# The residual sum of a layer stays in its PSUM bank; ScalarE copies it to x, and VectorE multiplies the bank with the scale row

## What is computed

```
def rmsnorm(x, g):
    y = x * rsqrt(mean(x * x, -1) + 1e-6) ; return y * g

for l in range(2):
    sh1, sc1, g1, sh2, sc2, g2 = split(silu(c) @ ada_w[l] + ada_b[l], 6)
    h = rmsnorm(x, norm1_g[l]) * (1 + sc1) + sh1
    x = x + g1 * hybrid_mixer(h, ...)        # ends with y @ w_out
    h = rmsnorm(x, norm2_g[l]) * (1 + sc2) + sh2
    x = x + g2 * swiglu(h, ...)              # ends with (...) @ w_ffn_out
return rmsnorm(x, final_g)
```

## Time and profile before

| | us |
|---|---|
| median of 3 runs | 1493.08 (1492.28 to 1493.75) |
| profiled execution, its own time | 1497.33 |
| its span in the trace | 1495.5 |
| TensorE busy | 1457.5 (97% of the span) |
| GpSimd busy | 1203.5 (80%) |
| VectorE busy | 785.5 (53%) |
| ScalarE busy | 739.3 (49%) |

### The profile page before, as it was taken

The page is one execution under the profiler, slowest core; times in us unless marked ns, Lnnn a source line. Parts: engine busy times, 40 slices in busy tenths (PEclk is TensorE's granted clock), DMA queues, the critical chain, the costliest instruction groups (busy, mean ns, idle before and its releaser), DMA issues.

```text
span 1495.5 us, 21644 instructions
## 1 busy us (share of the span) xinstructions
PE 1457.5 (97%) x7666; PEld 1218.3 (81%) x7666; DVE 785.5 (53%) x1582; ACT 739.3 (49%) x1222; POOL 1203.5 (80%) x968
## 2 busy tenths in 40 slices
PE   7999999999999999999999999999999999999997
PEld 3898777799977987778788887878888887788886
DVE  7667754766658758745466204264650043655302
ACT  3335675544444444764544445464654345455431
POOL 4799989888887977559898988907999977279994
PEclk9999999999999999999999999999999999999999
DMA  9995557688874996337666565714556757155651
GB/s 357 387 335 176 177 170 229 214 300 310 304 267 138 398 320 191 107 102 228 219 237 202 194 200 168 227 52 146 192 190 198 218 154 225 43 169 198 197 193 60
DMA packets 149685, 313.87 MB, mean 210 GB/s; under 512 B 10933, under 2 KB 31817, under 8 KB 149577
## 3 DMA queue, kind: packets, MB, share of 16 engines
q1 hardware_dynamic: 147824, 311.15, 62.1%
q10 hardware_dynamic: 1754, 1.35, 0.3%
HBM read 311.39 MB, written 1.06 MB: 209 GB/s over the span
## 4 chain that ended last, share of the span: by engine, by line
PE 86%; DVE 9%; ACT 2%; issue 1%; POOL 1%; DMA 0%; SPq 0%; DVEq 0%; ACTq 0%
PE bank L720 53%; PE bank L763 12%; PE bank L764 8%; PE bank L761 5%; DVE bank L1606 2%; PE bank L949 1%; PE bank L928 1%; POOL lo_units L676 1%; PE bank L965 1%; ACT hi_units L1190 1%; PE bank L908 1%; PE bank L799 1%; DVE bank L1527 1%; PE bank L851 1%; PE bank L1000 0%
## 5 line engine op out<-in xcount | busy, mean ns | idle before, releaser
L676 POOL TENSOR_TENSOR lo_units<-raw_units,hi_units 128x512 fp32r<-128x512 f32 (+3 forms) x928 | 1153.5, 1277 | 257.0 <-ACT hi_units L1190 255.9
L1190 ACT ACTIVATE hi_units<-raw_units 128x1024 fp32r<-128x1024 f32 (+1 forms) x470 | 483.3, 1031 | 437.3 <-PE bank L720 276.4
L720 PE MATMUL bank<-hi_units,turned 128*128 128x512 f32 (+3 forms) x1600 | 439.9, 390 | 1.5 <-DVE turned L1575 1.2
L720 PEld LDWEIGHTS bank<-hi_units,turned 128*128 128x128 f32 x1600 | 294.0, 189 | 53.0 <-issue 2.5
L764 PE MATMUL bank<-turned,lo_units 128*128 128x256 f32 x1024 | 288.2, 281 | 0.0
L720 PE MATMUL bank<-hi_units,turned_wide 128*128 128x512 f32 x992 | 275.5, 392 | 0.0
L763 PE MATMUL bank<-turned,hi_units 128*128 128x512 f32 x736 | 260.6, 399 | 0.0
L720 PE MATMUL bank<-lo_units,turned 128*128 128x512 f32 (+3 forms) x800 | 253.7, 384 | 1.5 <-POOL lo_units L676 1.3
L720 PEld LDWEIGHTS bank<-hi_units,turned_wide 128*128 128x128 f32 x992 | 185.8, 188 | 38.7 <-issue 0.5
L764 PEld LDWEIGHTS bank<-turned,lo_units 128*128 128x128 f32 x1024 | 194.2, 190 | 0.2
L720 PEld LDWEIGHTS bank<-lo_units,turned 128*128 128x128 f32 x800 | 150.4, 189 | 31.6 <-POOL lo_units L676 4.8
(11 more groups left out here) (253 smaller groups left out, 1385.0 us busy)
## 6 DMA issues: line engine op xcount, KB each, us to landing
ada_units<-in_ada_w SPq DMA_DIRECT2D x88, 512.0 KB, 8.1
raw_units<-in_w_ffn_tiles SPq DMA_DIRECT2D x72, 512.0 KB, 5.3
raw_units<-in_mlp_w_out SPq DMA_DIRECT2D x64, 512.0 KB, 3.3
raw_units<-in_mlp_w_tiles SPq DMA_DIRECT2D x56, 512.0 KB, 3.3
raw_units<-in_w_in SPq DMA_DIRECT2D x56, 458.0 KB, 9.3
raw_units<-in_w_in SPq DMA_DIRECT2D x48, 512.0 KB, 6.1
raw_units<-in_w_ffn_out SPq DMA_DIRECT2D x44, 512.0 KB, 3.7
raw_units<-in_moba_w_qkv SPq DMA_DIRECT2D x24, 512.0 KB, 3.8
```

What stands on the lines that cost most here:

```text
L676: pool.tensor_tensor(LO[:, s, b, 0:w], RAW[:, u["slot"], b, 0:w], HI_[:, s, b, 0:w].bitcast(F32), ALU.subtract).then_inc(lo_ready.sem, lo_ ...
L720: ins = pe.matmul(BANK[2 * c["pair"] + t][:, 0:w], (A[a] if A is BT else A[:, a])[:, part, t * P:(t + 1) * P], W[:, s, b, 0:w], start=(i = ...
L1190: act.activation(HI_[:, s, 0:n, 0:w], RAW[:, u["slot"], 0:n, 0:w], ACT.Copy)\
```

## The change

In the three boundaries A, B and C the residual sum is written to the PSUM bank instead of to x in SBUF. ScalarE squares the bank (not x) and copies the bank to x with an activation of its own (`keep_rows`). The product with the scale row reads bank and scale row. For the first half it is written in place and waits until ScalarE has copied. For the second half it is written to bank `TP`, now for both row tiles behind the addition of the squares; ScalarE's copy waits for this product (both read the bank), and stands between `root` and `prep` in ScalarE's list. TensorE's wait for the second pair (by then due a whole product later) is for this product and for the copy. Boundary D does the same work as before.

```diff
@@ tensor: pair_free
+            if what in ("wout", "ffo") and half == [1]:
+                pe.wait_ge(drained.sem, drained.at((*c["before"], 1)))
+                pe.wait_ge(act_side.sem, act_side.at(("kept", ("n2", i) if what == "wout" else ("n1", i + 1), 1, 1)))
+                return
@@ scalar
+        def keep_rows(tag, half, banks, tiles):
+            for t in tiles:
+                act.activation(X[:, t, half * CW:(half + 1) * CW], banks[t][:, :], ACT.Copy)\
+                    .then_inc(act_side.sem, act_side.mark(("kept", tag, half, t)))
@@ scalar: across_norm
-                    squares(tag, 1, (rows, ("x", key, t)), (t,), pair_banks(key) if tag == "final" else None)
+                    squares(tag, 1, (rows, ("x", key, t)), (t,), pair_banks(key))
                     root((tag, t), RSTD[:, t:t + 1], STAT[:, t:t + 1], 0, 1.0 / D)
+                    if tag != "final":
+                        act.wait_ge(drained.sem, drained.at((*key, t)))
+                        keep_rows(tag, 1, pair_banks(key), (t,))
@@ scalar: the first half (and the same for ffo, when a layer follows)
-            squares(("n2", l), 0, (drained, ("wout", l, 0)))
+            squares(("n2", l), 0, (drained, ("wout", l, 0)), banks=pair_banks(("wout", l, 0)))
+            keep_rows(("n2", l), 0, pair_banks(("wout", l, 0)), range(NT))
@@ vector: across_rms
-                bank, xs = pair_banks(key)[t][:, :], X[:, t, CW:2 * CW]
-                say(v.tensor_tensor(bank if coef is None else xs, xs, bank, ALU.add), ("x", key, t))
+                bank = pair_banks(key)[t][:, :]
+                say(v.tensor_tensor(bank, X[:, t, CW:2 * CW], bank, ALU.add), ("x", key, t))
...
-                if t:
-                    add_squares()
-                if coef is not None:
-                    ins = v.tensor_tensor(second[:, :], X[:, t, CW:2 * CW], MOD[:, coef + CW:coef + 2 * CW], ALU.mult)
-                    if t:
-                        tell(ins, drained, key)
-                    else:
-                        link(ins)
                 if t == 0:
                     dve.wait_ge(act_side.sem, act_side.at(("squares", tag, 0)))
-                    add_squares()
+                add_squares()
+                if coef is not None:
+                    ins = v.tensor_tensor(BANK[TP][:, :], second[:, :], MOD[:, coef + CW:coef + 2 * CW], ALU.mult)
+                    tell(ins, drained, (*key, t))
                 reciprocal_root(tag, t)
-                for half, bank in ((0, first), (1, second)):
+                for half, bank in ((0, first), (1, second if coef is None else BANK[TP])):
@@ vector: add_to_x
-                    ins = v.tensor_tensor(banks[t][:, :] if coef is None else xs, xs, banks[t][:, :], ALU.add)
+                    ins = v.tensor_tensor(banks[t][:, :], X[:, t, cc * CW:(cc + 1) * CW], banks[t][:, :], ALU.add)
                 tell(ins, drained, key)
                 after(key)
                 if coef is not None:
-                    scaled(cc, coef, to=banks)
+                    for t in range(NT):
+                        dve.wait_ge(act_side.sem, act_side.at(("kept", tag, cc, t)))
+                        ins = v.tensor_tensor(banks[t][:, :], banks[t][:, :], MOD[:, coef + cc * CW:coef + (cc + 1) * CW], ALU.mult)
+                    link(ins)
```

More of the change, by code:

```diff
@@ L595, in _ @@
                 if (l, c, i) == (1, 6, 0):
-                    sp.wait_ge(drained.sem, drained.at(("ffo", 0, 1)))
+                    sp.wait_ge(drained.sem, drained.at(("ffo", 0, 1, 1)))
                 if (l, c, i) in ((0, 10, 0), (1, 10, 0)):
@@ L1431, in _ @@
             prep_chunk(("ffo", l, 0))
-            squares(following, 0, (drained, ("ffo", l, 0)), banks=pair_banks(("ffo", l, 0)) if l + 1 == DEPTH else None)
+            squares(following, 0, (drained, ("ffo", l, 0)), banks=pair_banks(("ffo", l, 0)))
+            if l + 1 < DEPTH:
+                keep_rows(following, 0, pair_banks(("ffo", l, 0)), range(NT))
             across_norm(("ffo", l, 1), following, True, following if l + 1 < DEPTH else ("x", 0))
@@ L1600, in turn_lo_tile @@
                                  part[:, :, 0, :].bitcast(F32), ALU.subtract), turned_lo, (tag, "tile", n))
-        def scaled(half, coef, tiles=range(NT), to=None):
-            for t in tiles:
-                cols = slice(half * CW, (half + 1) * CW)
-                ins = v.tensor_tensor(to[t][:, :] if to else O[:, t, cols], X[:, t, cols], MOD[:, coef + half * CW:coef + (half + 1) * CW], ALU.mult)
-            link(ins)
         def root_of_squares(tag):
@@ L1991, in _, with add_to_x @@
             turn_lo(("y", l), AT, part=slice(2, 4))
-            def add_to_x(key, gain, factor, coef):
+            def add_to_x(key, gain, factor, tag, coef):
                 cc = key[-1]
@@ L2001, in add_to_x @@
                 for t in range(NT):
-                    xs = X[:, t, cc * CW:(cc + 1) * CW]
-                    ins = v.tensor_tensor(banks[t][:, :] if coef is None else xs, xs, banks[t][:, :], ALU.add)
+                    ins = v.tensor_tensor(banks[t][:, :], X[:, t, cc * CW:(cc + 1) * CW], banks[t][:, :], ALU.add)
                 tell(ins, drained, key)
@@ L2006, in add_to_x @@
                 if coef is not None:
-                    scaled(cc, coef, to=banks)
-            add_to_x(("wout", l, 0), 2 * D, 0.5, 4 * D)
+                    for t in range(NT):
+                        dve.wait_ge(act_side.sem, act_side.at(("kept", tag, cc, t)))
+                        ins = v.tensor_tensor(banks[t][:, :], banks[t][:, :], MOD[:, coef + cc * CW:coef + (cc + 1) * CW], ALU.mult)
+                    link(ins)
+            add_to_x(("wout", l, 0), 2 * D, 0.5, ("n2", l), 4 * D)
             across_rms(("wout", l, 1), 2 * D, 0.5, ("n2", l), 4 * D, 3 * D, ("n2", l))
@@ L2047, in _ @@
             following = ("n1", l + 1) if more else "final"
-            add_to_x(("ffo", l, 0), 5 * D, 1.0, D if more else None)
+            add_to_x(("ffo", l, 0), 5 * D, 1.0, following, D if more else None)
             across_rms(("ffo", l, 1), 5 * D, 1.0, following, D if more else None, 0,
```

## The result

The changed kernel takes 1497.22 us (median of 18 runs, 1494.07 to 1501.1); the kernel before, on the same chip and in turn with it, takes 1493.62 us (18 runs, 1490.3 to 1497.36). The ratio is 1.0023, with a 95% interval of 1.0014 to 1.0032: 3.4 us slower (2.1 to 4.8), where +0.1 us was forecast. The profiled execution took 1495.27 us, its span is 1493.5 us. That is less than the 1497.33 us of the profiled execution of before, although the median is more: one pair of profiles shows the opposite of what the timed runs show. This is the riddle of the case.

The account below looks back on a forecast made before the run. TensorE, busy 97% of the span, was taken as the bound. A 0.6 us lost, C 1.9 lost and B 2.4 gained gave +0.1 us, so a median of 1493.2 us, range 1489.5 to 1496.6.

Parts of the forecast that it names:

- the term for B: At boundary B, the net of earlier start, faster clock and added delays: 2.4 us gained.
- Part 1: Product reading a bank isn't held by GpSimd, 0.70 us each: gain 1.4 us at A, 2.6 at B, 0.1 at C.
- Rival 4: Product of bank and row is held by GpSimd too; boundaries lose about 2 us each: 1499 us; chance 0.02.
- Part 2: At B, with the 2.57 us wait cut, TensorE runs at 2.4 instead of 1.2 GHz: 1.55 us more gain.
- Parts 3 and 4: At tile 0, root to `o_rows` grows by 0.34 us; ScalarE's copy makes the next high part 1.02 us later.
- Part 5: The addition of tile 1's squares misses a GpSimd gap, 1.05 us at A and C; r is tile 0's root start.
- Rival 1: Tile 1's addition slips into the earlier GpSimd gap: A and C 1.05 us better each, B 0.5; 1490.6 us; chance 0.20.
- rival 2: At the boundaries tile 1 costs nothing, TensorE not waiting for unit 3: 4.7 us faster, 1488.4 us; chance 0.12.
- Rival 3: Granted clock falls to 0.50 behind idle time at A and C, 1.55 us each: 1496.3 us; chance 0.11.

Follow-up runs that it names:

- e11: The kernel before, no edit, one more profiled execution to see what boundary B usually takes: B took 11.10 us.
- e13: The kernel before, no edit, another profiled execution to look at boundary B: B took 8.54 us, the pair L1606 there 2.67 us.

## Why the prediction was wrong

**What failed: the term for B, in parts 1 and 2.** The prediction took 2.6 us of lateness and 1.55 us of slow clock at B, both from one execution, and put a gain of 2.4 us into the sum. That execution was the slowest at B of the six: 12.67 us against a mean of 10.42. With the hold gone and nothing added behind it B takes 8.55 us (the first half alone), so the two terms together were worth 4.1 us in that execution and 1.9 on average. Against them stand parts 3 to 5, which cost 10.34 - 8.55 = 1.8 us at B, as forecast. So the mean gain at B is 10.42 - 10.34 = 0.1 us, not 2.4, and the sum reads 0.6 + 1.9 - 0.1 = +2.4 us, which is the table's; from the 1493.62 us of the comparison that makes 1496.0, with 1497.22 measured (2.1 to 4.8 us slower). Carrying the sum from the profiled execution over to the median by subtracting a constant of 4.25 us was the place to notice: the profiled execution was that much slower than the median for some reason, and the term at B was 2.3 us of it.

**Part 1, the mechanism,** was right: the product of bank and row takes 0.65 us twice at all three boundaries, beside GpSimd too, and the idle time ahead of tile 0 went from 1.34 to 0.25 us at A and from 2.57 to 0.25 at B. Rival 4, that it is held like L1606, is refuted by the row at 443.99.

**Part 2** is right for that execution and wrong as a cost of the kernel: in e11 the same 2.57 us of idle time left the clock at 1.00, and B took 12.67 - 11.10 = 1.57 us less, which is the 1.55 of the prediction. It was paid in one execution of six.

**Parts 3 and 4** came within 0.02 us: at A the first `o_rows` product starts 272.26 - 271.33 = 0.93 us behind the root (0.94 forecast), the high part 1.23 us behind it (1.22), and the second low part of unit 3 comes 283.72 - 278.78 = 4.94 us behind the root of tile 1 (4.92). Only the split of TensorE's waits was off: the turning waits 0.94 us as said (0.9), the two low parts 0.58 and 0.27 instead of 1.0 and 0.6.

**Part 5,** the most doubtful step, was right too. The addition missed GpSimd's gap and took 1.27 us at A and at C, 0.72 at B (here B and C of the changed kernel):

```profile
473.52 0.72 DVE L1689 TENSOR_TENSOR small<-small 128x1 f32<-128x1 f32 x1
...
714.90 1.27 DVE L1689 TENSOR_TENSOR small<-small 128x1 f32<-128x1 f32 x1
```

The root of tile 1 came at r + 7.45 (7.42 forecast) and at B at r + 6.9 (6.85). Rival 1 is refuted by these rows, rival 2 by the waits on tile 1. The step from a margin of 0.06 us held in all five executions of the changed kernel, as A is 11.23 or 11.24 in each.

**Rival 3,** the clock at A and C, does occur, in one execution of six at each, and costs 1.7 us when it does (1.55 forecast), so some 0.3 us on average at each. Both kernels lose 4.6 and 5.1 us to such stretches in all, a difference that these executions don't tell from nothing. At A the idle times ahead of tile 1 are alike in the six executions (0.94 or 0.95 us before the turning, 0.57 or 0.58 before the first low part) and the clock fell in one, so their size alone does not decide it.

**The range** ended at 1496.6 because it took in the uncertainty of parts 3 to 5, which was small, and rivals 1 and 3, but none of the term at B, which was the largest of the sum and came from a single event. A B of "nothing to 2.4 us" would have moved its upper end to about 1499.

What stays open: what decides whether the pair is held for 22 to 24 us or slips through in 2.7, why the clock sometimes falls behind an idle time and sometimes not, and the last 0.3 us of A and C alone, whose own profile has a stretch of slow clock behind A. With the first half at B alone that boundary is 1.9 us shorter and the timed runs 0.7 us, with an interval that holds both that and nothing.

## What to carry to other kernels

A wait that ends with another engine's long row of work has no fixed size: before its removal is written into a sum, look at it in several executions, and let the profiled execution's distance from the median warn which term may be luck. Ahead of a PSUM-to-SBUF copy that only has to be done some time, put everything that feeds the bounding engine: here one copy ahead of the high parts turned a gain of 2.5 us into a loss of 2.7. And a sum of two small numbers held by a neighbour may be written with one operand as a scalar for each partition, which was not held.

## What the runs showed of the hardware

A VectorE instruction with both inputs in SBUF, beside an unbroken row of 32 GpSimd instructions, was held until the last of them in five executions of the kernel before (22.4 to 24.0 us for the pair) and not in the sixth (e13), nor in that of the kernel changed at A and C alone (2.67 and 2.80 us), whose GpSimd rows took 40.7 us instead of 39.8. The Trainium skill (SBUF — State Buffer, "Who interferes with whom") calls it an exclusive lock on a shared port pair, under which one waits until the other's instruction finishes. The 2.7 us agree with that, since a GpSimd instruction takes 1.26 us; the 22 us of the other executions don't.

With both inputs in SBUF but one element a partition, `tensor_tensor` was held to the end of GpSimd's current instruction (1.27 us), and as `tensor_scalar` with the second input as a scalar for each partition it took 0.21 us at the same place.

The time of one execution of an unchanged kernel varies by some 7 us (1490.3 to 1497.36), and 3.4 to 6.8 us of its six profiled executions went to stretches at a granted clock of 0.50 (1.2 GHz) ahead of TensorE's last product, each worth 1.7 us or twice that. Two idle times of 2.57 us at the same place gave 0.50 behind one and 1.00 behind the other.
